# Instruction orders changed at seven places of a three-block network kernel

## The chip, the cores and the metric

One core of a Trainium2 chip runs the whole program. The metric is the device time of one execution in microseconds. TensorE (PE) multiplies matrices, ScalarE (ACT) and VectorE (DVE) do element-wise work, GpSimd (POOL) does small arithmetic and issues some loads, SyncE (SP) issues the loads of the weights.

## The reference

The input has 256 tokens of 1024 features, all in float32. A first network of two layers runs, each layer being a half-weighted feed-forward block, a mixer (latent attention in layer 0, attention with forget gates in layer 1), a second feed-forward block and a gated embedding. A second block with pooling and dilated attention follows. Cut to what matters here:

```python
for i in range(2):
    h = h + 0.5 * swiglu(rms_norm(h, g_ffn1[i]), ffn1_w_in[i], ffn1_w_out[i])
    hn = rms_norm(h, g_mix[i])
    h = h + (mla_mixer(hn, ...) if i == 0 else fox_mixer(hn, ...))
    h = h + 0.5 * swiglu(rms_norm(h, g_ffn2[i]), ffn2_w_in[i], ffn2_w_out[i])
    h = h + sigmoid(rms_norm(h, g_ple[i]) @ ple_w_gate[i]) * (p[i] @ ple_w_proj[i])
# mla_mixer: z = hn @ w_in; q latents (512), key latents (256), k_pe (32)
#   q = rms_norm(c_q) @ w_uq; kv = rms_norm(c_kv) @ w_ukv; causal attention; @ w_o
# fox_mixer: q, k, v and 16 gate logits from hn @ w_in; decay = cumsum(log_sigmoid(f))
#   logits + decay[t] - decay[s]; causal attention; @ w_o
# second block: z = rmsnorm(x) @ w_in_2, pooling branch, dilated attention, gates, @ w_out_2
```

## The kernel before

**Products in three passes.** Every float32 weight is split into a rounded high part and a rest, both in a faster type: `hi*hi`, `lo*hi` and `hi*lo` are summed in PSUM (lines 628 to 630). ScalarE makes the high part `wh` from the loaded `raw` (`split`, line 1538), VectorE the low part `wl` as `raw - wh` (line 2086). Weights come in 205 groups of at most 128 x 2048 numbers through a ring of four buffers. The semaphore `hi_done` counts finished high parts, `lo_done` low parts (group g is usable at `lo_done` g - 1, since the first two groups go through finer pieces), and `w_used` counts groups that TensorE is done with. `split_to(n)` makes all parts up to group n - 1. `split_halves` (line 1559 on ScalarE) cuts one group in two, with `hi_half` and `lo_half` counting first halves.

**Order.** Nothing is scheduled by a tool: each engine's program is a list written out by hand, and an engine runs its own list strictly in that order. A wait holds up everything behind it on its engine.

**Norms.** The activations are scaled by the norm's gains only; the reciprocal root `rstd` multiplies later, when a product leaves PSUM. ScalarE sums squares (line 1570), GpSimd makes the root from them (`inverse_rms`, lines 2931 and 2932).

**First stage** (`f0`). TensorE takes groups 0 to 3 for the first two column chunks, then group 4 and on. ScalarE's list is: pieces, squares, high part of group 3, SiLU of chunk 0 (line 1633, for which `scaled` waits for `rstd`), high parts of groups 4 and 5, SiLU of chunk 1, and so on. GpSimd first waits for the eighth piece of weights, issues eight small loads (constants and tables, lines 2943 to 2951), and then makes the two roots. VectorE uses the tables in `angles_reduced` (line 2152), after chunk 1.

**Latent attention** (`mla`). TensorE makes the key latents and `k_pe` (288 columns), then the query latents from groups g + 2 and g + 3. Inside the latter, `turn_latents(range(4, 6), q)` transposes the key latents `lat`, which VectorE copied (line 2302) from PSUM, once for each tile of 128 tokens. `between(t, k)` is called ahead of each slice k of 128 features; slice 4 is the first of group g + 3, and each slice is six products. ScalarE and VectorE then round the transposed latents (`lh`, line 1681; `ll`, line 2311). Later, `keys_values(1, 0)` on VectorE (line 443) copies keys and values and so frees the PSUM that the next query products wait for.

**Forgetting attention** (`fox`). The first fill of 512 columns is squared (line 1924) and copied to `qf` (line 1933) by ScalarE, tile by tile; the copies free the PSUM of the second fill. The gate logits go by `flT` (line 2671), a transpose, the scaled sum `fl` (lines 2675, 2679), a logarithm on ScalarE (lines 1909 to 1913), products with a triangular matrix (lines 1256 to 1258) and another transpose. `scale_heads` (line 2601) needs GpSimd's roots `hrs` (lines 2995, 2997), which need VectorE's sums `hss` (line 2590).

**Last block.** Group g + 33, the second of the pooling branch's output weights, is split by ScalarE and VectorE during column chunk 15, after the attention shares are combined.

## Time and profile before

| | us |
|---|---|
| median of 3 runs | 1302.85 |
| lowest and highest of them | 1302.75, 1304.57 |
| the profiled execution's own time | 1302.51 |
| its span from first to last instruction | 1300.7 |
| TensorE busy in it (matmuls) | 1283.2 |
| VectorE busy | 929.7 |
| ScalarE busy | 679.3 |
| GpSimd busy | 125.9 |

Times inside the program are counted from the span's start. Matmuls are pipelined: a record starts before the one ahead of it has ended, so the distance of starts is the pace, and a record's length is not. The releaser behind an arrow is the instruction or transfer that ended an engine's idle time.

### The profile page before, as it was taken

The page shows a single profiled execution, that of the slowest core. Times are in us where ns is not written, and L with a number is a line of the kernel's source. Part 1 is how long each engine was busy: PE and PEld are TensorE (multiplying, and loading weights), DVE is VectorE, ACT ScalarE, POOL GpSimd, SP SyncE. Part 2 cuts the span into 40 slices and gives each one's busy share as a digit, 9 for nine tenths or more (in the row PEclk, how much of TensorE's full clock was granted, in tenths as well). Part 3 has the DMA queues.
Part 4 walks back from the last instruction along what each step waited for, and adds up shares of the span by engine and source line. Part 5 has one row for each costly group of instructions (what it writes and reads, how often), then busy time and mean ns, then how long its engine had stood idle before and what let it go on. Part 6 is the DMA issues. An engine that isn't in the chain of part 4 may idle for free.

```text
span 1300.7 us, 16758 instructions
## 1 busy us (share of the span) xinstructions
PE 1283.2 (99%) x6242; PEld 1057.4 (81%) x6242; DVE 929.7 (71%) x1298; ACT 679.3 (52%) x976; POOL 125.9 (10%) x190
## 2 busy tenths in 40 slices
PE   9999999999999999999999999999999999999997
PEld 6888888888888888888887777888888887788886
DVE  6878948986678956677875677667895656655674
ACT  7444537755444546544445567644444735566542
POOL 1000003711000000000001230000000133200000
PEclk9999999999999999999999999999999999999999
DMA  9665645228565655666564643466564496445541
GB/s 311 216 201 189 210 140 203 66 82 263 191 194 194 202 186 162 195 194 194 194 196 158 231 162 119 149 194 194 194 226 154 170 293 215 156 137 179 174 149 33
DMA packets 149505, 236.29 MB, mean 182 GB/s; under 512 B 10080, under 2 KB 104464, under 8 KB 148928
## 3 DMA queue, kind: packets, MB, share of 16 engines
q1 hardware_dynamic: 144432, 222.26, 52.6%
q0 software_dynamic: 4640, 12.81, 3.3%
q8 instruction: 39, 0.64, 0.2%
q10 hardware_dynamic: 368, 0.37, 0.1%
q14 instruction: 26, 0.21, 0.0%
HBM read 233.27 MB, written 4.47 MB: 183 GB/s over the span
## 4 chain that ended last, share of the span: by engine, by line
PE 91%; DVE 4%; ACT 3%; issue 1%; POOL 0%; DMA 0%; POOLq 0%; SPq 0%; ACTq 0%; DVEq 0%
PE acc L628 20%; PE acc L630 20%; PE acc L629 20%; PE acc L661 7%; PE acc L662 7%; PE acc L665 7%; PE misc L704 4%; DVE wl L2086 1%; ACT wh L1538 1%; PE misc L1339 1%; PE misc L888 1%; PE misc L1195 1%; ACT xh L1584 0%; PE acc L868 0%; ACT hn L1570 0%
## 5 line engine op out<-in xcount | busy, mean ns | idle before, releaser
L2086 DVE TENSOR_TENSOR wl<-raw,wh 128x2048 fp32r<-128x2048 f32 x199 | 450.6, 2270 | 183.5 <-ACT wh L1538 182.8
L1538 ACT ACTIVATE wh<-raw 128x2048 fp32r<-128x2048 f32 x205 | 383.5, 1894 | 125.3 <-PE acc L665 104.2
L628 PE MATMUL acc<-wh,xh 128*128 128x512 f32 (+1 forms) x832 | 324.5, 390 | 3.3 <-DVE xl L2132 1.6
L630 PE MATMUL acc<-wh,xl 128*128 128x512 f32 (+1 forms) x832 | 322.5, 388 | 0.0
L629 PE MATMUL acc<-wl,xh 128*128 128x512 f32 (+1 forms) x832 | 322.3, 387 | 0.0
L628 PEld LDWEIGHTS acc<-wh,xh 128*128 128x128 f32 x832 | 156.2, 188 | 36.7 <-DVE wl L2074 1.8
L630 PEld LDWEIGHTS acc<-wh,xl 128*128 128x128 f32 x832 | 156.2, 188 | 32.2
L629 PEld LDWEIGHTS acc<-wl,xh 128*128 128x128 f32 x832 | 156.2, 188 | 31.1
L1633 ACT ACTIVATE sg<-acc,rstd 128x256 f32<-128x256 f32 x88 | 41.4, 475 | 240.4 <-PE acc L630 240.3
L2252 DVE STREAM_TRANSPOSE aT<-a_n 32x384 f32<-32x384 f32 (+1 forms) x256 | 137.1, 536 | 3.9
L661 PE MATMUL acc<-wh,ah 128*128 128x512 f32 x320 | 124.8, 390 | 0.0
L662 PE MATMUL acc<-wl,ah 128*128 128x512 f32 x320 | 124.5, 389 | 0.0
L628 PE MATMUL acc<-wh,zh 128*128 128x512 f32 x272 | 108.6, 399 | 0.5 <-DVE zl L2132 0.5
L630 PE MATMUL acc<-wh,zl 128*128 128x512 f32 x272 | 106.2, 390 | 0.0
L629 PE MATMUL acc<-wl,zh 128*128 128x512 f32 x272 | 106.0, 390 | 0.0
L665 PE MATMUL acc<-wh,al 128*128 128x512 f32 x320 | 98.5, 389 | 0.0
L2931 POOL TENSOR_SCALAR rstd<-ssq 128x1 f32<-128x1 f32 x19 | 9.4, 493 | 886.3 <-ACT hn L1570 886.2
L2238 DVE SCALAR_TENSOR_TENSOR a_n<-acc,rstd,sg 128x256 f32<-128x256 f32 x88 | 42.0, 483 | 48.1 <-ACT sg L1633 48.1
L1584 ACT ACTIVATE xh<-misc,gains 128x128 fp32r<-128x128 f32 x128 | 40.2, 365 | 68.4 <-PE misc L704 60.2
L665 PEld LDWEIGHTS acc<-wh,al 128*128 128x128 f32 x320 | 60.1, 188 | 12.5
L662 PEld LDWEIGHTS acc<-wl,ah 128*128 128x128 f32 x320 | 60.1, 188 | 12.4
L661 PEld LDWEIGHTS acc<-wh,ah 128*128 128x128 f32 x320 | 60.1, 188 | 12.3
(365 smaller groups left out, 1613.1 us busy)
## 6 DMA issues: line engine op xcount, KB each, us to landing
raw<-in_ffn_w_in_dram SPq DMA_DIRECT2D x170, 512.0 KB, 4.8
raw<-in_ffn_w_out_dram SPq DMA_DIRECT2D x88, 512.0 KB, 4.3
raw<-in_w_in_dram SPq DMA_DIRECT2D x64, 512.0 KB, 4.7
raw<-in_fox_w_in_dram SPq DMA_DIRECT2D x24, 512.0 KB, 4.2
raw<-in_ple_w_gate_dram SPq DMA_DIRECT2D x16, 512.0 KB, 4.4
raw<-in_mla_w_o_dram SPq DMA_DIRECT2D x8, 512.0 KB, 4.0
raw<-in_fox_w_o_dram SPq DMA_DIRECT2D x8, 512.0 KB, 4.4
raw<-in_w_out_dram SPq DMA_DIRECT2D x8, 512.0 KB, 4.4
```

The lines of the kernel that those rows point to most:

```text
L628: pe.matmul(dst, hi, rhs_h, start=first, stop=False)
L629: pe.matmul(dst, hi, rhs_l, start=False, stop=False)
L630: return pe.matmul(dst, lo, rhs_h, start=False, stop=last)
L661: pe.matmul(acc(q + n, t), xa, wh[:, s, r], start=st, stop=False)
L662: pe.matmul(acc(q + n, t), xa, wl[:, s, r], start=False, stop=False)
L665: mm = pe.matmul(acc(q + n, t), xb, wh[:, s, r], start=False, stop=en)
L704: return pe.transpose(M[0:rows, b, cols], src, m[:, :])
L1538: act.activation(wh[:, s, 0:n], raw[:, s, 0:n], ACT.Copy).then_inc(hi_done, 1)
L1633: act.activation(sg[:, c % 2, t, :], acc(q, t)[:, 0:256], ACT.Silu, scale=rstd[:, t:t + 1]).then_inc(silu_done, 1)
L2086: dve.tensor_tensor(wl[:, s, 0:n], raw[:, s, 0:n], wh[:, s, 0:n].bitcast(F32), ALU.subtract)\
L2238: dve.scalar_tensor_tensor(a_n[:, (c // 3) % 2, t, w], acc(q, t)[:, 256:512], rstd[:, t:t + 1], sg[:, c % 2, t, :], ALU.mult, ALU.mult)\
L2252: e = dve.transpose(dst.rearrange("p c (t i r) -> p t c i r", t=NT, i=4)[:, :, :, i, :], src.rearrange("p t (c o r) -> p t c o r", o=4, r= ...
```

## The change

It changes seven places, all by the order in the engines' lists or by cutting one instruction in parts:

1. GpSimd's eight small loads wait for the second count of `lo_done` (the low part of group 3) in place of the eighth piece.
2. In `mla`, group g + 2 is rounded in three parts (512, 512 and 1024 columns) in place of two, and TensorE waits for the second part at slice 1.
3. The transposes of the key latents stand at slice 4, not 6, and group g + 4 is rounded in two halves with the rounding of the key latents between them.
4. On VectorE, `keys_values(1, 0)` stands between the two sums of the first queries.
5. In `fox`, ScalarE squares and copies the second tile of the first fill ahead of the high part of group g + 4; VectorE copies the gates (`flT`) ahead of that group's low part.
6. TensorE's gate products stand after the first slice of group g + 5 (six products), no longer ahead of that group; the gate transpose stands after its third slice, no longer after its second.
7. Group g + 33 of the last block is rounded in two halves.

The counts of `lo_half` that the gated embeddings wait for go up by two, since more first halves are counted ahead of them.

```diff
@@ TensorE, mla
+                if (t, k) == (0, 1):
+                    pe.wait_ge(lo_half, 2)
                 if (t, k) == (0, 2):
                     wait_group(g + 2)
-                if (t, k) == (0, 6):
+                if (t, k) == (0, 4):
                     turn_latents(range(4, 6), q)
@@ TensorE, ple
-                        pe.wait_ge(lo_half, 2 if name == "p0" else 3)
+                        pe.wait_ge(lo_half, 4 if name == "p0" else 5)
@@ TensorE, fox: after the products of slice j, and no longer after half groups
+                            if (w, j) == (5, 0):
+                                pe.wait_ge(forget_in, 2)
...
+                            if (w, j) == (5, 2):
+                                open_m(3, r[3] + 2)
...
-                        if (w, half) == (4, 1):
-                            pe.wait_ge(forget_in, 2)
...
-                        if (w, half) == (5, 0):
-                            open_m(3, r[3] + 2)
@@ ScalarE
-            def split_halves():
+            def split_parts(*ends, between=None):
                 g = done[0]
                 s = g % RING
                 act.wait_ge(raw_in[s], raw_at(g))
                 act.wait_ge(w_used, g - RING + 1)
...
+                a = 0
+                for e in ends:
+                    act.activation(wh[:, s, a:e], raw[:, s, a:e], ACT.Copy)\
+                       .then_inc(hi_done if e == GC else hi_half, 1)
+                    if between and a == 0:
+                        between()
+                    a = e
                 done[0] += 1
@@ ScalarE, norm ahead of mla
-                        split_halves()
+                        split_parts(512, 1024, GC)
                         squares(r, 0)
                         split_to(done[0] + 1)
                         squares(r, 1)
@@ ScalarE, mla
-            split_to(g + 5)
-            round_latents(range(4, 6))
+            split_to(g + 4)
+            split_parts(GC // 2, GC, between=lambda: round_latents(range(4, 6)))
@@ ScalarE, fox, first fill
-                    if n == 0 and t:
-                        split_to(g + 5)
                     tile_ready(act, fill, t, g + w + 1)
...
                         act.activation(qf[:, t, 0:512], acc(q, t), ACT.Copy).then_inc(acc_read[q % 2], 1)
+                        if t:
+                            split_to(g + 5)
@@ ScalarE and VectorE, last block
+                    if w == 31:
+                        split_parts(GC // 2, GC)          # VectorE: split_parts(4, GC // 2, GC)
                     split_to(g + w + 3)
@@ VectorE: split_parts(first, *ends, between=None), as on ScalarE, each part behind its hi_half
-                    dve.wait_ge(hi_half, 1)
-                    split_halves()
+                    split_parts(1, 512, 1024, GC)
...
-            split_to(g + 5)
-            rest_latents(range(4, 6))
+            split_parts(3, GC // 2, GC, between=lambda: rest_latents(range(4, 6)))
...
-            for t in range(NT):
-                sum_queries(0, t)
+            sum_queries(0, 0)
             keys_values(1, 0)
+            sum_queries(0, 1)
...
+            dve.wait_ge(w_used, g + 3)
+            dve.tensor_copy(flT[:, :], acc(q + 1, 0)[0:2 * H, 0:S]).then_inc(acc_read[(q + 1) % 2], NT)
             split_to(g + 5)
             sum_heads(0)
-            dve.wait_ge(w_used, g + 3)
-            dve.tensor_copy(flT[:, :], acc(q + 1, 0)[0:2 * H, 0:S]).then_inc(acc_read[(q + 1) % 2], NT)
             scale_heads(0)
@@ GpSimd
             link(pool.memset(mhalf[:, :], -0.5))
-            pool.wait_ge(piece_in[DK - 1], 16)
+            pool.wait_ge(lo_done, 2)
             pool.dma_start(tri[:, :], I["c_mats"][1]).then_inc(small_in, 16)
```

The three places on which most rests, as the built programs have them. First GpSimd at the start of the program; `tri` to `posi` are the small loads, `rstd` the norm's roots, `ssq` the sums of squares. Before:

```order
L2941 MEMSET mhalf 128x32
L2943 DMA tri<-in_c_mats_dram 128x128 [waits piece_in7,p_step]
L2944 DMA causal_f<-in_c_mats_dram 128x128
L2946 DMA hraw<-in_head_gains_dram 64x4 x2
L2947 DMA rgain<-in_rope_gains_dram 128x64
L2949 DMA bf<-in_fox_b_f_dram 128x16
L2950 DMA freq<-in_c_freq_dram 128x16
L2951 DMA posi<-in_pos_dram 128x2
L2931 ISA
L2931 TENSOR_SCALAR rstd<-ssq 128x1 [waits sq_done]
L2932 TENSOR_TENSOR rstd<-rstd,mhalf 128x1 [waits p_step]
```

And now:

```order
L2965 MEMSET mhalf 128x32
L2967 DMA tri<-in_c_mats_dram 128x128 [waits lo_done,p_step]
L2968 DMA causal_f<-in_c_mats_dram 128x128
L2970 DMA hraw<-in_head_gains_dram 64x4 x2
L2971 DMA rgain<-in_rope_gains_dram 128x64
L2973 DMA bf<-in_fox_b_f_dram 128x16
L2974 DMA freq<-in_c_freq_dram 128x16
L2975 DMA posi<-in_pos_dram 128x2
L2955 ISA
L2955 TENSOR_SCALAR rstd<-ssq 128x1 [waits sq_done]
L2956 TENSOR_TENSOR rstd<-rstd,mhalf 128x1 [waits p_step]
```

The order is the same; the wait ahead of the loads is another, and the roots stand behind the loads in both. ScalarE's list at the same place isn't changed; it is shown as it was before, since it says what waits for `rstd`:

```order
L1538 ACTIVATE wh<-raw 128x2048 [waits raw_in3]
L1633 ACT_TABLE_LOAD [waits rstd_done]
L1633 ACTIVATE sg<-acc,rstd 128x256 [waits acc_ready]
L1633 ACTIVATE sg<-acc,rstd 128x256 [waits rstd_done,w_used]
L1538 ACTIVATE wh<-raw 128x2048 [waits w_used,raw_in0]
L1538 ACTIVATE wh<-raw 128x2048 [waits w_used,raw_in1]
```

The first row is group 3, the last two are groups 4 and 5. The second place is TensorE among the products of the query latents; `lat` are the copied latents, `acc_read1` counts VectorE's copies of them. Before, at slice 6:

```order
L628 MATMUL acc<-wh,xh 128x512
L629 MATMUL acc<-wl,xh 128x512
L630 MATMUL acc<-wh,xl 128x512
L704 MATMUL misc<-ident,lat 128x128 [waits m_read2,acc_read1]
L704 MATMUL misc<-ident,lat 128x128 x3
L628 MATMUL acc<-wh,xh 128x512
```

Now, at slice 4, where group g + 3 begins:

```order
L628 MATMUL acc<-wh,xh 128x512
L629 MATMUL acc<-wl,xh 128x512
L630 MATMUL acc<-wh,xl 128x512
L704 MATMUL misc<-ident,lat 128x128 [waits m_read2,acc_read1,lo_done]
L704 MATMUL misc<-ident,lat 128x128 x3
L628 MATMUL acc<-wh,xh 128x512
```

The four transposes moved ahead by twelve products, and now carry that group's own wait. The third place is ScalarE at the start of the forgetting attention; `sqf` are squares and `qf` copies of the first fill's two tiles, the first `wh` with `raw_in2` is group g + 4. Before:

```order
L1933 ACTIVATE qf<-acc 128x512 [waits acc_read1]
L1538 ACTIVATE wh<-raw 128x2048 [waits w_used,raw_in2]
L1924 ACTIVATE sqf<-acc 128x512 [waits w_used]
L1933 ACTIVATE qf<-acc 128x512
L1538 ACTIVATE wh<-raw 128x2048 [waits w_used,raw_in3]
L1909 ACTIVATE fl<-fl 128x32 [waits m_read3]
```

And now:

```order
L1936 ACTIVATE qf<-acc 128x512 [waits acc_read1]
L1927 ACTIVATE sqf<-acc 128x512 [waits w_used]
L1936 ACTIVATE qf<-acc 128x512
L1540 ACTIVATE wh<-raw 128x2048 [waits w_used,raw_in2]
L1540 ACTIVATE wh<-raw 128x2048 [waits w_used,raw_in3]
L1914 ACTIVATE fl<-fl 128x32 [waits m_read3]
```

Group g + 4's high part went from ahead of the second tile's square and copy to behind them.

## Rows read from the trace of the kernel before

**Rows 1.** The page: the chain that ended last, shares by engine.

```profile
PE 91%; DVE 4%; ACT 3%; issue 1%; POOL 0%; DMA 0%; POOLq 0%; SPq 0%; ACTq 0%; DVEq 0%
```

**Rows 2.** TensorE's waits: whom for, us in total, times, longest us.

```profile
PE acc L628 <- DVE xl L2132: 1.6, 1, 1.6
...
PE acc L628 <- ACT qf L1933: 0.9, 1, 0.9
...
PE acc L628 <- DVE wl L2086: 0.5, 2, 0.3
...
PE acc L628 <- DVE wl L2124: 0.5, 1, 0.5
...
PE acc L628 <- DVE vn L443: 0.4, 1, 0.4
...
PE misc L704 <- DVE fl L2695: 0.3, 1, 0.3
```

**Rows 3.** TensorE's timeline at six places: start, us, instruction, [idle ahead <- releaser].

```profile
1.25 3.56 PE L608 MATMUL acc<-hn 128*128 128x512 bf16 x9 [1.25 <-DVE hn L2284]
...
30.77 0.39 PE L628 MATMUL acc<-wh,xh 128*128 128x512 f32 x1
...
203.10 0.39 PE L628 MATMUL acc<-wh,xh 128*128 128x512 f32 x1
...
205.83 0.60 PE L704 MATMUL misc<-ident,lat 128*128 128x128 f32 x4
...
706.76 0.39 PE L630 MATMUL acc<-wh,xl 128*128 128x512 f32 x1
...
721.68 0.40 PE L1256 MATMUL misc<-fl,tri 128*128 128x16 f32 x2 [0.15 <-DVE fl L2691]
...
722.37 0.48 PE L628 MATMUL acc<-wh,xh 128*128 128x512 f32 x1
```

**Rows 4.** GpSimd's timeline, 14 to 22 us.

```profile
14.69 0.76 POOL L2943 DMA_DIRECT2D tri<-in_c_mats_dram  x1 [13.84 <-DMA raw<-in_ffn_w_in_dram]
...
18.68 0.54 POOL L2951 DMA_DIRECT2D posi<-in_pos_dram  x1
20.08 0.18 POOL L2931 TENSOR_SCALAR rstd<-ssq 128x1 f32<-128x1 f32 x1 [0.86 <-ACT hn L1570]
20.34 0.57 POOL L2932 TENSOR_TENSOR rstd<-rstd,mhalf 128x1 f32<-128x1 f32 x1
```

**Rows 5.** ScalarE's timeline in the first stage and in the forgetting attention.

```profile
20.91 1.91 ACT L1538 ACTIVATE wh<-raw 128x2048 fp32r<-128x2048 f32 x1
22.84 1.28 ACT L1633 ACT_TABLE_LOAD   x1
...
24.86 1.92 ACT L1538 ACTIVATE wh<-raw 128x2048 fp32r<-128x2048 f32 x1
...
706.92 1.92 ACT L1538 ACTIVATE wh<-raw 128x2048 fp32r<-128x2048 f32 x1
...
709.20 0.61 ACT L1933 ACTIVATE qf<-acc 128x512 f32<-128x512 f32 x1
```

**Rows 6.** VectorE's timeline in the first stage and in both attentions.

```profile
22.85 2.29 DVE L2086 TENSOR_TENSOR wl<-raw,wh 128x2048 fp32r<-128x2048 f32 x1 [2.86 <-ACT wh L1538]
...
26.82 2.29 DVE L2086 TENSOR_TENSOR wl<-raw,wh 128x2048 fp32r<-128x2048 f32 x1 [0.89 <-ACT wh L1538]
...
32.85 0.17 DVE L2152 MEMSET ones<- 128x128 f32 x1
...
204.09 0.48 DVE L2302 TENSOR_SCALAR lat<-acc,rstd 128x256 f32<-128x256 f32 x1
...
227.25 1.81 DVE L2344 TENSOR_REDUCE hss<-sqb 128x8 f32<-128x768 f32 x2 [0.96 <-ACT sqb L1719]
...
717.90 2.28 DVE L2086 TENSOR_TENSOR wl<-raw,wh 128x2048 fp32r<-128x2048 f32 x1
```

**Rows 7.** DMA issues of the first 50 us: KB each, us to landing.

```profile
posi<-in_pos_dram POOLq DMA_DIRECT2D x1, 1.0 KB, 6.1
```

More of the change, by code:

```diff
@@ L1242, in _ @@
                                     mm.then_inc(acc_ready, 1)
+                            if (w, j) == (5, 0):
+                                pe.wait_ge(forget_in, 2)
+                                open_m(3, r[3] + 1)
+                                pe.matmul(M[:, 3, 0:H], tri[:, :], fl[:, 2, 0, :], start=True, stop=True)
+                                pe.matmul(M[:, 3, H:2 * H], ones[:, :], fl[:, 2, 0, :], start=True, stop=False)
+                                pe.matmul(M[:, 3, H:2 * H], tri[:, :], fl[:, 2, 1, :], start=False,
+                                          stop=True).then_inc(m_ready[3], 1)
+                            if (w, j) == (5, 2):
+                                open_m(3, r[3] + 2)
+                                turn(3, slice(0, P), fl[:, 0, :, :].rearrange("p t h -> p (t h)"), NT * H)\
+                                    .then_inc(m_ready[3], 1)
                         if half:
@@ L1252, in _ @@
                             mm.then_inc(m_ready[3], 1)
-                        if (w, half) == (4, 1):
-                            pe.wait_ge(forget_in, 2)
-                            open_m(3, r[3] + 1)
-                            pe.matmul(M[:, 3, 0:H], tri[:, :], fl[:, 2, 0, :], start=True, stop=True)
-                            pe.matmul(M[:, 3, H:2 * H], ones[:, :], fl[:, 2, 0, :], start=True, stop=False)
-                            pe.matmul(M[:, 3, H:2 * H], tri[:, :], fl[:, 2, 1, :], start=False,
-                                      stop=True).then_inc(m_ready[3], 1)
-                        if (w, half) == (5, 0):
-                            open_m(3, r[3] + 2)
-                            turn(3, slice(0, P), fl[:, 0, :, :].rearrange("p t h -> p (t h)"), NT * H)\
-                                .then_inc(m_ready[3], 1)
             def o_rows(j, t, halves=(0, 1)):
@@ L1562, in split_halves @@
                 act.wait_ge(w_used, g - RING + 1)
-                for n in range(2):
-                    w = slice(n * GC // 2, (n + 1) * GC // 2)
-                    act.activation(wh[:, s, w], raw[:, s, w], ACT.Copy).then_inc((hi_half, hi_done)[n], 1)
+                a = 0
[5 more added lines that the diff above has]
+                    a = e
                 done[0] += 1
@@ L2126, in split_halves, with split_parts @@
                 done[0] += 1
+            def split_parts(first, *ends, between=None):
+                g = done[0]
+                s = g % RING
+                a = 0
+                for n, e in enumerate(ends):
+                    if e == GC:
+                        dve.wait_ge(hi_done, g - 1)
+                    else:
+                        dve.wait_ge(hi_half, first + n)
+                    dve.tensor_tensor(wl[:, s, a:e], raw[:, s, a:e], wh[:, s, a:e].bitcast(F32), ALU.subtract)\
+                       .then_inc(lo_done if e == GC else lo_half, 1)
+                    if between and a == 0:
+                        between()
+                    a = e
+                done[0] += 1
             def rest_x(name, r, t, k, n):
@@ L2821, in _ @@
                     w = 2 * c + k
+                    if w == 31:
+                        split_parts(4, GC // 2, GC)
                     split_to(g + w + 3)
```

## The prediction

> **What bounds the kernel now.** I read the chain of work that ended last first: 91% of it is TensorE [rows 1]. So TensorE sets the end, and an edit pays only by what TensorE waits for. The list of TensorE's waits therefore comes second [rows 2]; its lines hold all that orders on other engines can give back. A product's record lasts 0.39 us, while products of 512 columns start every 0.23 us (twelve from 203.10 to 205.83) [rows 3]: a pause of pace is about 0.16 us longer than the listed idle time. So corrected, the stops that this diff goes at are: the first stage's group 3 (part of the two `wl L2086` entries, 0.4), the input projection of the latent attention (`wl L2124`, 0.65), its query fills (`vn L443`, 0.5), the forgetting attention's second fill (`qf L1933`, 1.05) and its two gate steps (0.15 of idle time ahead of `L1256` [rows 3] and `fl L2695`, so 0.3 and 0.4), and the last block's output weights (the other `wl L2086`, 0.4). Together 3.7 us, or 0.28%: all that can be won. Third, I followed in the timelines of the other engines who is in a queue behind each moved step.
>
> **Small loads later.** GpSimd issues eight small loads itself, between 14.69 and 18.68 + 0.54 = 19.22, so 4.5 us of its queue, and only then works out the first norm's reciprocal roots: from 20.08 to 20.34 + 0.57 = 20.91 [rows 4]. Now it waits, ahead of the loads, for the second count of `lo_done`; that is VectorE's low part of weight group 3, which ends at 22.85 + 2.29 = 25.14 [rows 6]. The norm's roots stand behind the loads in the same queue. They come at 25.2 + 4.5 + 0.83 = 30.55, in place of 20.91. ScalarE waits for exactly these: its first SiLU needs them, the wait stands ahead of the table load, and the high part of group 4 is queued behind. From the table load at 22.84 to group 4's start at 24.86 it takes 2.02 us [rows 5]; from there the high part and VectorE's low part, which ends at 26.82 + 2.29 = 29.11, take 4.25 us [rows 5, 6]. So group 4 is ready at 30.55 + 2.02 + 4.25 = 36.8, and with the hand-over at 36.9. The second root comes 0.83 after the first and is there before the second SiLU. TensorE starts group 4 at 30.77 [rows 3]. **This is a new stop of 6.2 us.** If the table load of 1.28 us were done ahead of the wait, it would be 4.9; if every load took as long to issue as the first one (0.76), it would be 7.8. I take 6.2, since the eight issues as a whole were timed. Group 5's low part follows in 2.3 us, ahead of the 5.4 us that TensorE needs for group 4, so the stop is not repeated.
>
> The stop at group 3 isn't helped: ScalarE's high part of it runs from 20.91 with no idle time ahead [rows 5], so it waited for no transfer. It would be swallowed by the new one anyhow: 0. The last load lands 6.1 us after its issue [rows 7], now at about 35.4; VectorE asks for it at 32.85 [rows 6], but this step moves behind group 5 too, to about 40, so that costs nothing.
>
> **What the pause does to the clock.** The longest idle time from which TensorE now comes back is 1.6 us (`xl L2132`) [rows 2]. At the program's start, after longer rest, nine products of 512 columns take 3.56 us [rows 3], where nine at full pace and the last one's record take 8 x 0.23 + 0.39 = 2.2 us: part of them runs at 1.2 GHz and not 2.4, and that costs 1.4 us. No row shows a rest of 6 us. Its cost lies between 0 and twice the start's, 2.8. Since 6.2 us is four times the longest rest that left the pace alone, I take the start's price, **1.4 us**. The Trainium skill, page "TensorE: Matmul & The Clock Gate", section "Part 1: The HAM clock gate", says that a TensorE that has rested falls back to 1.2 GHz and gets 2.4 GHz again only by sustained work; it speaks for the same side and against this edit, and by it the sum would be the one with the 1.4 us.
>
> **Key latents.** The input group is now cut in three parts, so its first 512 columns are ready earlier and the stop of 0.65 goes. But the transposes of the key latents move ahead by twelve products, from 205.83 to the place of 203.10 [rows 3]. They read what VectorE's copy of the second tile's latents writes, and that ends at 204.09 + 0.48 = 204.57 [rows 6]; it hangs on the norm's second root, which hangs on ScalarE's squares, and nothing in the change brings those ahead (the extra cut puts them back by some 0.1). TensorE arrives there 0.65 sooner, at 202.45, and waits until about 204.7. Behind that come the transposes and the twelve products that were ahead of them (12 x 0.23 = 2.7): their end is at 207.4 + the transposes, where it was at 205.83 + the transposes. **Net +1.6 us** (the won 0.65 is in it). The rounding of the latents between two weight halves, which this was to serve, isn't waited for then: its work ends while TensorE still does the delayed products.
>
> **Query fills.** Two sums of 1.81 us stood ahead of the copies that TensorE waits for [rows 6]; one of them, 0.9, now stands behind. The stop of 0.5 goes. Whether a later step gives it back is open, since the head loop waits for GpSimd's roots: 0 to -0.5, taken -0.4, as the copies were bound by VectorE's queue alone.
>
> **Forgetting attention.** ScalarE now copies the second tile ahead of group 4's high part. The tile's last product ends at 706.76 + 0.39 = 707.15 [rows 3]; square and copy took about 1.0 us together (708.84 to 709.20 + 0.61) [rows 5], so the copy is done at 708.2. The stop ended with that copy at 709.8 and was 1.05 long, so TensorE comes at 708.8 and the stop goes. Group 4's high part, at 706.92 before [rows 5], starts at 708.15: 1.25 later. VectorE's low part, the sums, GpSimd's roots, the scaling and then group 5's low part follow in one chain. That last one ran from 717.90 to 720.18 [rows 6]; now it ends at 721.4. TensorE came to group 5 at 722.37 [rows 3]; without the stops, and with the gate products (721.68 to 722.37, 0.7) [rows 3] moved behind six products of group 5, it comes at 722.37 - 1.05 - 0.3 - 0.7 = 720.3 and waits 1.1. The gate's logarithm and its copy are 1.25 later as well, so by my estimate from the same rows the moved gate steps wait 0.1 and 0.4 again. Won 1.75, given back 1.6: **-0.1**, between -1.0 and +0.5. The early copy of the gates fills VectorE's idle time and costs nothing.
>
> **Output weights.** In two halves, VectorE starts after half of ScalarE's 1.92 us [rows 5]; the low part is complete some 0.9 earlier, more than the stop. **-0.4**, with plain products behind it to the end.
>
> **Sum.** Against the profiled execution's own 1302.51 us: +6.2 + 1.4 + 1.6 - 0.4 - 0.1 - 0.4 = +8.3, so 1310.8. The median of the runs is 0.3 above that execution: **1311.0**.
>
> **Rivals.** (a) The pause is there but the clock stays: 1309.6. For it: no row shows a fall after a rest inside the program. (b) The pause is there, but the orders behind it hold what they promise: the transposes find their latents, and the forgetting attention keeps its 1.7. That takes 2.2 + 1.6 from the sum: 1307.2. For it speaks that the copy of the latents has idle time ahead of it, against it that the idle time was ended by ScalarE and the norm's roots. (c) The other side: the roots' delay doesn't reach TensorE. ScalarE's group 4 has slack from 29.11 to 30.77, 1.66 us; so this decides at roots that come by 22.84 + 1.7 = 24.5. The wait alone opens at 25.14, so it could only be if the loads' issues didn't hold up the arithmetic behind them. Then there is no pause and no clock loss, 1310.8 - 7.6 = 1303.2 by the execution, 1303.5: not slower. (d) Besides (c), the transposes don't wait and every stop goes: 1302.85 - 3.7 = 1299.1, faster.
>
> **How the numbers follow.** Forecast 0.50, (a) 0.32, (b) 0.08, (c) 0.06, (d) 0.04. A measurement of this kernel tells some 0.2% (2.6 us) from no change. Slower by more than that: forecast, (a) and (b), 0.90; within: (c), 0.06; faster: (d), 0.04. The range goes from 1306.8, which is (a) with the shortest pause (4.9) and the forgetting attention at its best (-1.0), and a little below (b), to 1313.2, with 2.8 for the clock and the longer ends of the smaller terms. It holds the forecast, (a) and most of (b).
>
> **What would show it.** In the profile after: GpSimd's first load at about 25.2 and its first `rstd` at about 29.8; ScalarE idle between 22.8 and 30.5 until `rstd`; TensorE idle from about 31 to 37 with the low part of group 4 as releaser, and products 0.43 us apart behind it for some microseconds. At the key latents, TensorE waits about 2.2 us for VectorE's `lat` ahead of four transposes. In the forgetting attention no wait for `qf`, but about 1 us ahead of group 5 for `wl`. No wait at the output weights. Wrong would be: a first `rstd` near 21 us, or a SiLU that runs without it; a granted clock of 2.4 GHz right behind the pause (then (a)); transposes that start at once.

## The result, and the profile after

The changed kernel takes 1315.97 us (median of 6; 1314.15 to 1316.69), the kernel before 1302.8 us (median of 6): ratio 1.0093, 95% interval 1.0083 to 1.0103. So it is slower, by 13.2 us. The profiled execution of it took 1314.15 us (span 1312.4), 11.6 us more than the profiled one of before. The profiled execution of the kernel with early loads took 3604.99 us and isn't read; that kernel's numbers below are those of its other eight.

**The start.** First GpSimd's timeline (start, us, instruction, [idle ahead <- releaser]), in answer to [rows 4]:

```profile
26.20 0.76 POOL L2967 DMA_DIRECT2D tri<-in_c_mats_dram  x1 [25.35 <-DVE wl L2093]
...
30.19 0.54 POOL L2975 DMA_DIRECT2D posi<-in_pos_dram  x1
30.87 0.18 POOL L2955 TENSOR_SCALAR rstd<-ssq 128x1 f32<-128x1 f32 x1
31.14 0.57 POOL L2956 TENSOR_TENSOR rstd<-rstd,mhalf 128x1 f32<-128x1 f32 x1
```

Then ScalarE's and VectorE's, in answer to [rows 5, 6], and TensorE's, in answer to [rows 3]:

```profile
31.78 1.28 ACT L1638 ACT_TABLE_LOAD   x1 [8.53 <-POOL rstd L2956]
...
33.80 3.71 ACT L1540 ACTIVATE wh<-raw 128x2048 fp32r<-128x2048 f32 x2
```

```profile
23.28 2.29 DVE L2093 TENSOR_TENSOR wl<-raw,wh 128x2048 fp32r<-128x2048 f32 x1 [2.86 <-ACT wh L1540]
...
35.74 4.49 DVE L2093 TENSOR_TENSOR wl<-raw,wh 128x2048 fp32r<-128x2048 f32 x2 [1.29 <-ACT wh L1540]
```

```profile
30.97 0.39 PE L630 MATMUL acc<-wh,xl 128*128 128x512 f32 x1
38.18 0.77 PE L628 MATMUL acc<-wh,xh 128*128 128x512 f32 x1 [6.83 <-DVE wl L2093]
38.75 0.63 PE L629 MATMUL acc<-wl,xh 128*128 128x512 f32 x1
```

The chain is the predicted one link by link: loads behind the low part of group 3 (the first of VectorE's rows), the roots behind the loads, the table load behind the root, group 4 behind that. Its first product starts at 38.18, 6.99 us later than the pace ahead of it would have it. Behind it products start 0.43 us apart until 43.0. The table of stretches (length, busy time of the engines, then the granted clock as a share of 2.4 GHz, DMA share, GB/s) shows why:

```profile
core 0: us, PE busy (x) PEld busy (x) DVE busy (x) ACT busy (x) POOL busy (x), PEclk, DMA share, GB/s
31.00:38.00 7.00, 0.36 (x2) 0.00 (x0) 3.13 (x4) 6.21 (x7) 1.37 (x4) 0.87 0.31 11
38.70:43.00 4.30, 4.30 (x11) 3.30 (x10) 4.02 (x13) 3.14 (x2) 0.00 (x0) 0.50 0.86 265
43.50:46.00 2.50, 2.50 (x13) 2.07 (x12) 2.40 (x4) 0.00 (x0) 0.00 (x0) 1.00 0.92 313
```

0.50 is 1.2 GHz, and from 43.5 it is 2.4 GHz again. The same products, set side by side, are 0.43 us later than before ahead of the pause and 9.75 later behind the slow ones: 9.3 us for pause and clock, 7.0 and 2.3.

**TensorE's waits** of the whole execution (whom for, us in total, times, longest), in answer to [rows 2]:

```profile
PE acc L628 <- DVE wl L2093: 8.3, 3, 6.8
PE misc L704 <- issue: 2.2, 1, 2.2
...
PE misc L704 <- DVE nmx L2673: 1.3, 1, 1.3
...
PE misc L704 <- DVE fl L2717: 0.2, 1, 0.2
```

`qf`, `vn`, `wl L2124` and one `wl L2086` of [rows 2] are gone, as the change means it. New are 2.2 us at the key latents, 1.2 us for `wl` ahead of the forgetting attention's group 5 (in the first line, with the pause and 0.3 at group 3), and 1.3 us of idle time, a stop of 1.48, for `nmx`, the first softmax of that attention. The list puts the 2.2 down to "issue"; the rows of VectorE and TensorE there show for what it was. The transposes start when the second tile's latents are copied, 213.94 + 0.48 = 214.42:

```profile
213.94 0.48 DVE L2325 TENSOR_SCALAR lat<-acc,rstd 128x256 f32<-128x256 f32 x1
```

```profile
214.51 0.63 PE L704 MATMUL misc<-ident,lat 128*128 128x128 f32 x4 [2.19 <-issue]
```

**The first softmax**, which the prediction doesn't have. VectorE there needs the decay rows, which GpSimd writes to memory and reads back to all partitions. Before, then after, GpSimd's read and VectorE's first use of it:

```profile
734.53 1.15 POOL L3004 DMA_DIRECT2D decay<-decay_rows  x2 [1.91 <-DMA decay_rows<-crows]
...
744.09 0.29 DVE L2649 CUSTOM_DVE_ANT_0 prf<-misc,decay 128x128 f32<-128x128 f32 x1 [4.13 <-DMA decay<-decay_rows]
```

```profile
746.20 1.15 POOL L3028 DMA_DIRECT2D decay<-decay_rows  x2 [1.77 <-DMA decay_rows<-crows]
...
757.83 0.29 DVE L2671 CUSTOM_DVE_ANT_0 prf<-misc,decay 128x128 f32<-128x128 f32 x1 [7.42 <-DMA decay<-decay_rows]
```

The read takes 9.56 us before and 11.63 after, from its issue to VectorE's first use, and VectorE was idle for it in both. In the kernel before that cost TensorE nothing: its transposes behind the first softmax follow the products ahead of them at full pace. After, they wait (TensorE's rows, before, then after):

```profile
746.61 0.38 PE L704 MATMUL misc<-ident,qf 128*128 128x128 f32 x2
```

```profile
758.53 0.44 PE L704 MATMUL misc<-ident,qf 128*128 128x128 f32 x2 [1.32 <-DVE nmx L2673]
```

After, they start 0.70 us behind VectorE's first use of the rows, and so they do in the other profiled executions that wait there. Before, the first use at 744.09 would have let them start at 744.79: the rows came 1.8 us ahead of their need. What the DMA engines moved in these two stretches (mean rate; then by queue, q0 the read, q1 the weights: packets, MB, share of the engines):

```profile
DMA packets 925, 3.53 MB, mean 367 GB/s; under 512 B 64, under 2 KB 64, under 8 KB 669
...
q0 software_dynamic: 288, 2.10, 51.9%
q1 hardware_dynamic: 637, 1.43, 44.4%
```

```profile
DMA packets 1109, 4.17 MB, mean 360 GB/s; under 512 B 93, under 2 KB 93, under 8 KB 852
...
q1 hardware_dynamic: 820, 2.06, 49.4%
q0 software_dynamic: 288, 2.10, 43.1%
```

The rate is nearly the same and the read is the same 2.10 MB; 0.63 MB more of weights go through in the meantime. That alone does not tell cause from effect, since a longer stretch has room for more weights. The Trainium skill, page "DMA: Bandwidth & Descriptors", section "Issuing engines are not separate DMA queues", says that transfers of all issuing engines run interleaved on the same 16 DMA engines; the rows agree, with both queues at work in the same stretch (51.9 and 44.4% of the engines' time before, 43.1 and 49.4% after).

### The profile page after: what moved, and what is told of

Its sections match the earlier page's. It is cut to its first block, busy times and chain, and to the rows that moved or that the text cites. A ratio compares the mean times of both kernels' runs of the same rounds, so it can differ in the third digit from the quotient of the medians.

```text
span 1312.4 us, 16764 instructions
## 1 busy us (share of the span) xinstructions
PE 1285.4 (98%) x6242; PEld 1059.4 (81%) x6242; DVE 930.1 (71%) x1301; ACT 679.5 (52%) x979; POOL 125.0 (10%) x190
## 4 chain that ended last, share of the span: by engine, by line
PE 89%; DVE 3%; ACT 2%; POOL 2%; DMA 1%; issue 1%; POOLq 0%; SPq 0%; ACTq 0%; DVEq 0%
PE acc L628 20%; PE acc L630 20%; PE acc L629 19%; PE acc L661 7%; PE acc L665 7%; PE acc L662 7%; PE misc L704 4%; DVE wl L2093 1%; DMA decay<-decay_rows 1%; ACT wh L1540 1%; PE misc L1341 1%; PE misc L888 1%; POOL hrs L3021 1%; PE misc L1197 0%; POOL rt L2996 0%
## 5 line engine op out<-in xcount | busy, mean ns | idle before, releaser
L2093 DVE TENSOR_TENSOR wl<-raw,wh 128x2048 fp32r<-128x2048 f32 (+1 forms) x197 | 445.9, 2270 | 181.2 <-ACT wh L1540 180.4
L1540 ACT ACTIVATE wh<-raw 128x2048 fp32r<-128x2048 f32 (+1 forms) x203 | 379.5, 1894 | 122.1 <-PE acc L665 104.1
```

What stands on the lines that cost most here:

```text
L1540: act.activation(wh[:, s, 0:n], raw[:, s, 0:n], ACT.Copy).then_inc(hi_done, 1)
L2093: dve.tensor_tensor(wl[:, s, 0:n], raw[:, s, 0:n], wh[:, s, 0:n].bitcast(F32), ALU.subtract)\
```

## Experiments

Spans are those of profiled executions; where two kernels are set side by side, it is product by product on TensorE.

**Roots ahead of the loads.** The changed kernel with

```diff
+            norm(0)
             pool.wait_ge(lo_done, 2)
             pool.dma_start(tri[:, :], ...
 ...
-            norm(0)
             norm(1)
```

> GpSimd works out the first norm's two roots ahead of the eight small loads; the loads still wait for VectorE's low part of group 3, and all the rest of the change stays. Theory, the roots are the link: the first root is done at about 21 us as in the kernel before, TensorE starts group 4 with no stop (6.99 us in the changed kernel's trace), products behind it start 0.23 us apart at once, so the 2.3 us of slow pace go too. Span 1312.4 - 7.0 - 2.3 = 1303.1 us, time about 1305, with the loads landing at about 35 us and nobody waiting for them. Rival, the late loads themselves do it (their landing, or their traffic beside the weights'): the stop stays and the time is within 2 us of the changed kernel's 1316.

Measured: span 1303.0, median 1306.86 us of 11 (lowest 1304.72). GpSimd's timeline:

```profile
20.58 0.56 POOL L2956 TENSOR_TENSOR rstd<-rstd,mhalf 128x1 f32<-128x1 f32 x1
...
25.59 0.77 POOL L2968 DMA_DIRECT2D tri<-in_c_mats_dram  x1 [3.52 <-DVE wl L2093]
```

The loads are as late as in the changed kernel, the pause and the slow products are gone. The theory holds: not the late loads cost, but what stands behind them in GpSimd's queue.

**Loads early.** The changed kernel with

```diff
-            pool.wait_ge(lo_done, 2)
+            pool.wait_ge(piece_in[DK - 1], 16)
```

> The small loads wait for the last input piece again, as in the kernel before; all the rest of the change stays. Theory: the same span as with the roots ahead of the loads, 1303.1 us, within 0.6, so late loads are worth nothing by themselves; against the kernel before +2.4 us of span, which is -0.6 at the input projection, +2.3 for the key latents, -0.5 at the query fills, -1.1 at the forgetting attention's second fill, +1.4 ahead of its group 5, +1.5 at its first decay rows and -0.4 at the output weights. Rival, the late loads free the first weight transfers: TensorE's stop at group 3 (0.41 us) goes when they are late and is back here, and this kernel is slower than the other one by 0.4 us or more.

Measured: lowest 1304.70, median 1306.65 us of 8, against 1304.72 and 1306.86 with the roots ahead. Late loads win nothing: this kernel isn't slower, and the stop at group 3 is 0.42 us in the kernel above, whose loads are late, and 0.41 before. Place by place the theory isn't shown, since no profile of this kernel is read.

**Pool's line alone.** The kernel before with the wait changed to `lo_done`, 2:

> The kernel before with one line changed: GpSimd's small loads wait for the low part of group 3. Theory: the stop of 7.0 us ahead of group 4 and 2.3 us of slow products behind it, nothing else: the span of a profiled execution is 1310.0 us where before it was 1300.7, the lowest time about 1311.7. Rival, part of the price belongs to the other parts (the cuts and orders behind): under 8 us.

Measured: span 1310.9, 10.2 above before, median 1312.28 us of 4 (lowest 1311.01). The stop is 6.97 us, and 13 products behind it are slow, 2.97 us, where the changed kernel had 10 and 2.34. With 0.4 us that lie ahead of the pause this is 10.3: nothing else in the program moves by more than 0.1.

**Busy in the pause.** The changed kernel with, in TensorE's program ahead of group 4,

```diff
+                    if g0 == 0 and c == 2:
+                        for _ in range(29):
+                            pe.matmul(M[:, 0, :], xh[:, 0, 0:P], xh[:, 0:2, :].rearrange("p k s -> p (k s)"),
+                                      start=True, stop=True)
```

> The changed kernel with 29 more products of 512 columns, which nobody reads, ahead of group 4, into a PSUM bank that is free there (29 x 0.23 = 6.7 us): TensorE works through the pause, and the roots come as late as before. Theory, the rest lowers the clock and that costs 2.3 us behind the pause: group 4 starts at the same 38 us, its products start 0.23 us apart from the first on, and the time is 2 to 3 us below the changed kernel's 1316. Rival, the slow products behind the pause come from the weights' arrival or from VectorE's lateness: the time is within 0.7 us of the changed kernel's, with products 0.43 us apart as there.

Measured: span 1311.0, median 1312.96 us of 4. Group 4 starts at 38.30, and its products are 0.23 us apart at once. Set side by side, 2.26 us are won there: the slow products come from the rest, not from late weights. But 1.57 are lost again behind the 2.19 us of rest at the key latents, where the changed kernel's own execution ran on at full pace:

```profile
207.00:209.80 2.80, 2.80 (x15) 2.29 (x13) 2.10 (x1) 2.42 (x7) 1.01 (x1) 1.00 0.79 275
213.60:216.60 3.00, 3.00 (x9) 2.33 (x8) 2.67 (x5) 2.60 (x3) 0.00 (x0) 0.50 0.14 55
217.00:219.00 2.00, 2.00 (x10) 1.64 (x9) 0.99 (x1) 0.00 (x0) 0.00 (x0) 1.00 0.87 180
```

**Busy in both pauses.** The kernel above with 11 such products ahead of the transposes of the key latents too:

> The changed kernel with products that nobody reads in both pauses: 29 ahead of group 4, and 11 (2.5 us) ahead of the transposes of the key latents, where TensorE else rests for 2.2 us. In the kernel that was busy in the first pause alone, six products behind the second one were 0.43 us apart and cost 1.2 us; in the changed kernel's own trace none. Theory, a rest of 2.2 us lowers the clock in some executions: with both covered there are no products 0.43 us apart behind either place, the lowest time is about 1311.8 and the median at most 1 us above. Rival, the slow products there were an accident of that execution and not of the rest: the time is the same as with the first pause covered alone, 1312.4 to 1313.

Measured: span 1308.6, median 1311.16 us of 4 (lowest 1310.4). No slow product behind either place. It is 1.4 us better than expected, for a reason of its own: here the decay rows landed 8.4 us after their issue and the stop for `nmx` wasn't there.

**Transposes back.** Loads early, and

```diff
-                if (t, k) == (0, 4):
+                if (t, k) == (0, 6):
                     turn_latents(range(4, 6), q)
```

> Small loads as in the kernel before, and besides it the transposes of the key latents stand behind six slices of the input group again, not four; the cut of that group in three and the rounding between weight halves stay. Theory, the transposes wait for VectorE's copy of the second tile's latents (2.35 us of stop): 2.3 us less than with the small loads alone put back, so a span of about 1300.8 us, and no wait of TensorE at the transposes. Rival, the moved transposes only take a wait that else comes at the first key and value products: TensorE waits there for the rounded latents, and the span stays above 1302.5 us.

Measured: median 1305.23 us of 11 (lowest 1303.16, span 1301.3). The lowest is 1.56 below the roots-ahead kernel's, not 2.3. The profiled span is 1303.7, above the rival's 1302.5, but in an execution whose start was 1.9 us longer than the roots-ahead kernel's. TensorE's timeline at the first keys and values:

```profile
211.09 0.50 PE L628 MATMUL acc<-wh,lh 128*128 128x512 f32 x1 [0.37 <-DVE wl L2145]
...
214.31 1.09 PE L704 MATMUL misc<-ident,lat 128*128 128x128 f32 x8 [0.17 <-DVE lat L2351]
```

Theory and rival both have a share: the transposes no longer wait, but 0.53 + 0.33 us of stops come one and two steps later.

**Three parts alone.** The kernel before with the input group in three, one query sum behind the first keys and values, and the output weights in halves:

> The kernel before with three parts of the change alone: the input group of the latent attention cut in three, one query sum behind the first keys and values, and the output weights in halves. Small loads, key latents and the forgetting attention stay as before. Theory, these three only take stops away: 0.65, 0.5 and 0.4 us, so a profiled span of about 1299.2 us where before it was 1300.7, and a lowest time of about 1300.9. Rival, the won time comes back at the next wait, as in the kernel with the transposes put back, where 0.53 and 0.33 us of new stops stood at the key and value products: the lowest time is 1302 or more.

Measured: median 1301.67 against 1302.8 us (11 and 18 executions), ratio 0.9992, interval 0.9983 to 1.0001; lowest 1301.21. Product by product: -0.70 at the input projection, +0.62 back at the first keys and values, -0.61 at the query fills, -0.61 at the output weights. So the cut of the input group is worth 0.1 us: TensorE is early there, but the latents that it needs next hang on the norm and are not. The rival holds for this part, the theory for the other two.

**Forgetting attention alone.** The kernel before with only its order as the change has it:

> The kernel before with the forgetting attention's order alone changed, as the change has it. Theory: the stops of 1.05 and 0.34 us go; 1.38 ahead of group 5, 0.4 at the second gate step and 0.6 to 1.8 at the first decay rows come, so +1.0 to +2.2 us against the kernel before at the end of the forgetting attention, and 1303.3 to 1304.5 us for the lowest time. Rival, as the prediction had it, the later chain gives back only what the stops gave: within 0.5 us of the kernel before, with no stop at nmx.

Measured: median 1305.35 us of 10 (lowest 1303.98) against 1304.16 of 17 (lowest 1302.28). Product by product: -1.18 at the second fill, +1.06 from there until the gates are passed (a stop of 1.38 ahead of group 5 is in it), so -0.12 until there; then a stop of 1.73 us for `nmx`, and in this execution slow products behind it, together +3.74. The clock in that stretch:

```profile
751.20:754.70 3.50, 3.50 (x10) 2.67 (x10) 2.70 (x6) 2.48 (x9) 0.00 (x0) 0.51 0.22 59
```

**Decay rows in parts.** The changed kernel with the decay read in four parts, and VectorE waiting for the first heads alone:

```diff
-                    for n in range(NT):
-                        pool.dma_start(decay[:, n, :, :], bass.AP(decay_d, (1 - n) * H * P, [[0, P], [1, H * P]]))\
-                            .then_inc(decay_in, 16)
+                    for a, b, landed in ((0, 4, decay_in), (4, H, decay_rest)):
+                        for n in range(NT):
+                            pool.dma_start(decay[:, n, a:b, :],
+                                           bass.AP(decay_d, ((1 - n) * H + a) * P, [[0, P], [1, (b - a) * P]]))\
+                                .then_inc(landed, 16)
```

> The changed kernel with one difference: GpSimd reads the decay rows back in four parts, first those of heads 0 to 3 (a quarter of the bytes), then those of heads 4 to 15, and VectorE waits at the first softmax for the first quarter alone. Theory, the stop of 1.48 us for nmx is the landing of that read (11.6 us after its issue, 9.6 in the kernel before), which now shares its time with weight transfers: the first nmx comes some 5 us sooner, the stop is gone, and the span is 1.2 to 1.5 us below that of the changed kernel, with everything ahead of it the same. Rival, TensorE is held there by VectorE's queue or by ScalarE's exponentials: the first nmx comes sooner and a stop of over 0.8 us stays at the same transposes.

Measured: median 1313.91 us of 5 (lowest 1312.22), span 1311.2. VectorE's first use of the rows, and TensorE's transposes behind it:

```profile
754.89 0.29 DVE L2674 CUSTOM_DVE_ANT_0 prf<-misc,decay 128x128 f32<-128x128 f32 x1 [4.01 <-DMA decay<-decay_rows]
```

```profile
757.53 0.38 PE L705 MATMUL misc<-ident,qf 128*128 128x128 f32 x2
```

The first quarter is used 8.1 us after the issue (746.80) in place of 11.6, and the stop is gone: set against the kernel before, the changed kernel loses 1.89 us at this place, this one none. The rows came 3.5 us sooner after their issue and not 5, but the theory holds: nothing else held TensorE there. The span is 1.2 us lower and not 1.9, mostly since twelve products were slow behind the pause and not ten (2.82 us in place of 2.34).

**Mended forgetting attention.** The three parts, the change's order, and on VectorE

```diff
             sum_heads(0)
-            scale_heads(0)
+            split_to(g + 6)
             dve.wait_ge(m_ready[3], f[3] + 1)
             ...
+            scale_heads(0)
```

and the copy of the decay rows ahead of the key scaling:

> The same three parts, and in the forgetting attention the change's order (second tile copied ahead of group 4's high part, gates copied early, gate products inside group 5), mended behind it: VectorE works out the low part of group 5 and the gates ahead of the query scaling, in its idle time, and copies the decay rows ahead of the key scaling, so that they are written about 1 us sooner. Theory, TensorE's 1.38 us ahead of group 5, 0.4 at the gate and 1.5 at the first decay rows are what the late low part and the late decay rows cost: all three go, and with the stop of 1.05 the span is 1.0 to 1.8 us below that of the three parts alone, so 1297.4 to 1298.2. Rival, the decay rows, which go through memory and land 9 to 11 us after their issue, set the time of the first softmax however the rest is ordered: a stop of over 1 us stays there for nmx and the span is within 0.7 us of the three parts alone.

Measured: median 1299.67 against 1302.8 us (8 and 18 executions), ratio 0.9974, interval 0.9964 to 0.9985; lowest 1299.13, 2.1 below the three parts. The profiled execution, at 1301.24 the slowest of the eight, shows the rival: no stop ahead of group 5 nor at the gates (-2.0 us until there), but 1.26 us for `nmx`. The rows are written 3.0 us sooner than before (728.99), but in this execution the write took 3.9 us to the issue of the read, in place of 2.5, and the read 11.9, in place of 9.6.

**All that helps.** The kernel above with the decay rows in parts, and six products that nobody reads ahead of the first real one:

> The kernel with the three parts and the mended forgetting attention, and two things more: the decay rows read in four parts as above, and six products that nobody reads ahead of the program's first real product, where TensorE else rests for 1.5 to 2.3 us for the first input. Theory: no stop for nmx, so no execution has the 1.3 us of it, and no execution starts with products 0.43 us apart (which in the executions profiled here came with rests of 2.1 us and more at that place and cost up to 2 us): the lowest time is 1298.5 to 1299.2 as in the mended kernel, the highest at most 1 us above, where that had 2.1. Rival, the slow start has nothing to do with the rest: times still lie in two clusters some 2 us apart.

Measured: 1299.58 to 1300.53 us, median 1300.1 of 7 against 1304.16 of 17 in the same series; ratio 0.9969, interval 0.9958 to 0.998. TensorE waits for nothing between 700 and 760 us. The seven times lie within 0.95 us, as expected, but the lowest is 0.4 above the bound, and above the mended kernel's. It beats both kernels; against the median of the 75 executions of before in all series, 1302.85, it is 2.75 us.

**Where the median's further 1.8 us lie.** The changed kernel once more:

> The changed kernel once more, for a second profiled execution. Theory, its time varies from one execution to the next because three rests lie near the point at which the clock falls: the start (1.3 to 2.5 us of rest), the pause ahead of group 4 (always slow behind it, 2.3 to 2.8 us lost) and the key latents (2.2 us of rest, 0 to 1.2 us lost), so between 1314.0 and 1317.5 us; the profiled span is 1312.4 us plus what of slow products stands at the start and behind the latents. Rival, the median's excess of 1.8 us over the first profiled execution lies elsewhere: the span differs by over 1 us with no slow products at these places.

Measured: 1313.96, 1314.06 and 1318.69 us; the profiled one of these, 1314.06, has the same places and sizes as the first (stop for `nmx` 1.56, ten slow products behind the pause). It decides nothing: the two executions profiled are both of the short kind. Of the nine executions three took 1313.96 to 1314.15 and six 1315.24 or more. The kernel before does the same: 47 of 75 took 1302.28 to 1303.40, 28 took 1304.01 or more, with nothing between. So, with the rest at the start filled:

> The changed kernel with six products that nobody reads ahead of the program's first real product, in place of the rest there. Theory, the rests that the change adds (2.2 us at the key latents, 1.2 and 1.5 us in the forgetting attention) lower the clock in some executions for about ten products, 1 to 2.3 us each time: with the start covered the times still spread over 2 us or more, from about 1314 to 1317 us. Rival, the spread and the median's excess are all from the start, as in the kernel before: the times lie within 1 us of one another, near 1314.2.

Measured: 1313.27 to 1314.37 us, median 1314.3 of 5. The theory, that the change's new rests spread the times, isn't seen here; the rival fits: with the start covered, the upper times are gone and the median is that of the profiled execution. It rests on these five times alone, since no long execution of the changed kernel was profiled, and the next kernel spreads again. What a start of the other kind looks like is in the execution of the transposes-back kernel, then in that of before:

```profile
7.40:9.80 2.40, 2.40 (x6) 1.78 (x7) 1.90 (x5) 1.12 (x3) 0.00 (x0) 0.55 1.06 351
```

```profile
6.80:9.00 2.20, 2.16 (x11) 1.84 (x12) 1.37 (x4) 1.80 (x5) 0.00 (x0) 1.00 0.99 321
```

Six products against eleven, at 0.55 and at 1.00 of the clock; ahead of the first TensorE was idle for 2.12 us, ahead of the second for 1.59. It isn't the length of the rest alone: in the execution of the forgetting attention's order alone the products at the start were as slow, until 9.8 us, behind 0.94 us of idle time, and in that of the roots-ahead kernel they ran at full pace behind the same 0.94 us and the same slow products ahead of it. The granted clock reads 1.00 in both (7.2 to 9.8), so there the pace alone tells the two apart.

With the start, the key latents and the decay rows covered:

> The changed kernel with products that nobody reads at the start (6) and ahead of the transposes of the key latents (11), and with the decay rows read in four parts, so that only the pause ahead of group 4 and the 1.2 us ahead of group 5 of the forgetting attention are left as rests. Theory, the rests at these three places cause the spread: the times lie within about 1 us of one another, and near the lowest that the changed kernel gives without the stop for the decay rows, 1312.2 to 1313.2 us; the pause still costs its 7.0 + 2.3 to 2.7 us. Rival, the spread comes from the pause (how long the products behind it stay slow) or from what no record shows: it stays at 2 us or more.

Measured: 1312.04 to 1314.04 us, median 1312.36 of 5. The level is as expected, the spread of 2.0 isn't: the profiled execution (1313.27) had twelve slow products behind the pause, 2.80 us where the changed kernel's had 2.34, so some 0.5 us of the spread are the pause's own; the rest is open. So covering the start doesn't always take the spread away.

## Why the prediction was right and where it failed

The sign, and the cause of most of it, were right; the time was 5 us too low. By its own terms, in the profiled execution:

| term | predicted | measured |
|---|---|---|
| pause ahead of group 4 | +6.2 | +7.0 |
| clock behind it | +1.4 | +2.3 (2.3 to 3.0 in five others) |
| key latents | +1.6 | +1.5 |
| query fills | -0.4 | -0.6 |
| forgetting attention | -0.1 | +1.8 |
| output weights | -0.4 | -0.6 |
| start, not of the change | 0 | +0.4 |
| sum | +8.3 | +11.8 (TensorE's last product: +11.7) |

**Pause: right in mechanism, 0.8 short.** Every link of the chain was named. The prediction had the first load at about 25.2, right behind the low part (25.14) [rows 6]; it starts at 26.20, where that low part ends at 23.28 + 2.29 = 25.57. So 0.6 us pass between the wait and the first issue, and 0.14 between the last load and the root, which the sum had at next to nothing. (By its own terms the stop was 36.9 - 30.77 = 6.1.)

**Clock: right in kind, mis-sized.** The term that was too small is the start's price [rows 3], taken for a rest of 6 us: 1.4 where the six profiled executions with the pause lost 2.3 to 3.0, though the range went to 2.8. That the start's products ran at 1.2 GHz was read from their pace; the granted clock of that stretch (1.20 to 5.00) reads 1.00 in the trace of before. Rival (a), a pause without a fall, is refuted by the granted clock of 0.50 and by the kernel that was kept busy. The Trainium skill, page "TensorE: Matmul & The Clock Gate", section "Part 1: The HAM clock gate", says that a TensorE that has rested falls back to 1.2 GHz; the trace agrees for this rest (0.50 behind 6.83 us of idle time).

**Key latents: right.** TensorE came 0.7 us sooner and waited 2.35 for the copy of the second tile's latents. What the text took for granted, that the cut of the input group wins its 0.65 for good, is wrong when done alone: 0.62 come back at the next step.

**Forgetting attention: the step that failed.** Up to the gates the working holds: 1.18 won at the second fill, 1.05 given back until the gates are passed; -0.13 against -0.1. The sum then ended there, "given back 1.6". But the prediction itself had found that the low part, the sums, the roots and the scaling are 1.25 us late "in one chain", and did not follow that chain on: through the key scaling, the copy of the decay rows, their way through memory, to the first softmax. There TensorE lost 1.9 us. VectorE's 4.13 us of idle time for that read stand in the trace of before; it cost TensorE nothing then, and so it was not looked at.

The chain's lateness alone would not have made that stop. Measured against TensorE's own products (10.45 us later there than before), the read was issued 1.2 us later than before, and the rows had come 1.8 us ahead of their need. The read itself took 2.07 us longer as well: 1.2 + 2.1 - 1.8 = 1.5, the stop. The other profiled executions fit: with the order of before the read took 9.5 to 9.8 us, with the change's order, mended or not, 10.7 to 11.9 where it wasn't cut in parts, with a stop each time; in the one where it took 8.4 (busy in both pauses) there was none. Why it takes longer is not shown. In the two kernels set side by side above more weights went through beside it, and in the read of 8.4 us they were 1.44 MB, about as many as before; no run changed the weight traffic alone.

**Median: the other step that failed, the last one.** "The median of the runs is 0.3 above that execution" carried over from the kernel before, where most executions are of the short kind. Six of nine executions of the changed kernel took 1.1 us and more above the profiled one, and with the start's rest filled none of five did. Whether six of nine is chance (28 of 75 for the kernel before) or the change's doing is open.

No single one of these steps put the time above the range. Without the 1.9 us of the first softmax the median would be 1314.1, without the median's excess of 1.5 over the prediction's 0.3 it would be 1314.5, and without both 1312.6, inside the range's 1313.2. That bound also left out a term that the prediction had named: its longer pause of 7.8 would have taken it to 1314.8. (The lower one, 1306.8, comes to 1307.4 from its own terms; nothing hangs on it.)

## What to carry to other kernels

Move a wait on an in-order engine only after reading the whole queue behind it: here eight small loads that nobody needed for long stood ahead of two tiny roots that everybody needed, and the cure was to swap them, not to time them. A stop that is taken away is won only if the next thing needed is early too; follow a chain that is made late up to the point where it is next asked for, through memory as well. And in front of a transfer that is just in time, cut it so that the part asked for first lands first.

## What the runs showed of the hardware

Products ran slow behind rests far shorter than the pause, and not each time. Behind 6.8 us of idle time they were slow in all six profiled executions that had it (10 to 13 products, 2.3 to 3.0 us, granted clock 0.50). Behind 2.19 us at the key latents they were slow in one execution (seven products) and not in five others with 2.18 or 2.19; behind 1.57 us at the decay rows in one (eight), where 1.32 us in the changed kernel left the pace alone; at the start behind 2.12 and 2.33 us, and in one execution behind 0.94, but not behind 0.94 in another nor behind 1.59 in the kernel before. The length of the rest alone doesn't tell which, and no run here shows what does. So a stop of two microseconds can cost twice its length (1.73 at the decay rows, 3.74 with the slow products behind it), and a median can lie where no profiled execution is.
